# A decoder trunk on one core: the mixer's instruction order, the engine of the pooling sums and the buffers of the second values

## The reference

```
h = x + 1/2 * postRMS(SwiGLU_1(preRMS(x)))
u = preRMS(h); a = u @ w_in
y = [conv_module(a_conv) | multiscale_pool(a_pool) | sparse_attention(a_q, a_k, a_v, a_qidx, a_kidx, a_widx)] @ w_out
h = h + postRMS(y)
h = h + 1/2 * postRMS(SwiGLU_2(preRMS(h)))
```

## Time and profile before

| | |
|---|---|
| runs | 1202.85, 1202.2 and 1207.68 us, median 1202.85 |
| profiled execution | 1207.4 us, span of its trace 1205.9 us |
| granted TensorE clock, mean | 0.958 of full speed |
| TensorE busy | 1112.4 us (92% of the span) |
| VectorE, ScalarE, GpSimd busy | 758.3, 529.6 and 220.4 us |
| bytes moved | 192.93 MB, mean 160 GB/s |
| first mixer | from about 220 to 395 us of the span, second from about 811 to 985 |

### The profile page before, as it was taken

The page is one execution under the profiler, slowest core; times in us unless marked ns, Lnnn a source line. Parts: engine busy times, 40 slices in busy tenths (PEclk is TensorE's granted clock), DMA queues, the critical chain, the costliest instruction groups (busy, mean ns, idle before and its releaser), DMA issues.

```text
span 1205.9 us, 28753 instructions
## 1 busy us (share of the span) xinstructions
PE 1112.4 (92%) x9404; PEld 1044.6 (87%) x9404; DVE 758.3 (63%) x1232; ACT 529.6 (44%) x854; POOL 220.4 (18%) x249
## 2 busy tenths in 40 slices
PE   5999999989579999999989999999885799999997
PEld 4999999877348899999989999998753699999995
DVE  3766644787854766664466666457788466666546
ACT  4444434521255544443454444345113555444335
POOL 3211100420600312110031111013224021211002
PEclk9999999999769999999999999999896799999999
DMA  7454566342553345555435456553336434555541
GB/s 248 170 204 169 196 230 225 114 124 98 105 151 128 106 174 187 178 189 177 157 91 194 179 196 225 207 193 109 103 105 111 131 123 157 182 183 183 183 174 39
DMA packets 92300, 192.93 MB, mean 160 GB/s; under 512 B 12338, under 2 KB 50418, under 8 KB 92098
## 3 DMA queue, kind: packets, MB, share of 16 engines
q1 hardware_dynamic: 89730, 187.44, 46.8%
q0 software_dynamic: 2496, 4.55, 1.7%
HBM read 189.35 MB, written 2.59 MB: 159 GB/s over the span
## 4 chain that ended last, share of the span: by engine, by line
PE 50%; issue 38%; DVE 3%; POOL 3%; ACT 2%; POOLq 2%; DMA 1%; DVEq 0%; ACTq 0%; SPq 0%
PE PS L999 14%; PE PS L1000 13%; PE PS L1001 13%; PE PS L1105 3%; PE PS L1033 2%; POOLq L1465 1%; PE PS L1044 1%; PE PS L1048 1%; PE PS L1045 1%; POOL h L1420 1%; ACT w_hi L356 1%; POOL pa L1472 1%; DVE w_lo L559 1%; DVE wk L684 1%; PE PS L1111 1%
## 5 line engine op out<-in xcount | busy, mean ns | idle before, releaser
L559 DVE TENSOR_TENSOR w_lo<-raw,w_hi 128x1024 fp32r<-128x1024 f32 x300 | 395.3, 1318 | 315.1 <-ACT w_hi L356 313.1
L356 ACT ACTIVATE w_hi<-raw 128x1024 fp32r<-128x1024 f32 x300 | 315.7, 1055 | 256.0 <-PE PS L1001 221.3
L999 PE MATMUL PS<-x_hi,w_hi 128*128 128x264 f32 x1456 | 417.0, 286 | 10.8 <-DVE w_lo L559 10.8
L1000 PE MATMUL PS<-x_lo,w_hi 128*128 128x264 f32 x1456 | 414.7, 285 | 0.0
L1001 PE MATMUL PS<-x_hi,w_lo 128*128 128x264 f32 x1456 | 414.3, 285 | 0.0
L999 PEld LDWEIGHTS PS<-x_hi,w_hi 128*128 128x128 f32 x1456 | 276.3, 190 | 12.0 <-DVE w_lo L559 11.7
L1000 PEld LDWEIGHTS PS<-x_lo,w_hi 128*128 128x128 f32 x1456 | 276.5, 190 | 0.1
L1001 PEld LDWEIGHTS PS<-x_hi,w_lo 128*128 128x128 f32 x1456 | 275.2, 189 | 0.0
L999 PE MATMUL PS<-h_hi,w_hi 128*128 (+1 forms) x832 | 237.1, 285 | 3.4 <-issue 3.0
L1001 PE MATMUL PS<-h_hi,w_lo 128*128 (+1 forms) x832 | 236.9, 285 | 0.0
L1000 PE MATMUL PS<-h_lo,w_hi 128*128 (+1 forms) x832 | 236.2, 284 | 0.0
(11 more groups left out here) (265 smaller groups left out, 1072.2 us busy)
## 6 DMA issues: line engine op xcount, KB each, us to landing
raw<-in_wts SPq DMA_DIRECT2D x315, 512.0 KB, 3.6
kv<-in_kT SPq DMA_DIRECT2D x128, 64.0 KB, 2.2
kx<-in_kxT SPq DMA_DIRECT2D x128, 32.0 KB, 2.1
kv<-in_vC SPq DMA_DIRECT2D x64, 64.0 KB, 1.9
vx<-in_vC POOLq DMA_DIRECT2D x32, 64.0 KB, 2.3
vx<-in_vC SPq DMA_DIRECT2D x32, 64.0 KB, 2.1
h<-in_xT SPq DMA_DIRECT2D x1, 1056.0 KB, 5.0
out_yT<-h SPq DMA_DIRECT2D x8, 132.0 KB, 1.7
```

Source lines behind the costliest of these rows:

```text
L356: act.activation(w_hi[:, u % SPLIT, :], raw[:, u % RAW, :], ACT.Copy) \
L559: tt(w_lo[:, u % SPLIT, :], raw[:, u % RAW, :], w_hi[:, u % SPLIT, :].bitcast(F32), AL.subtract) \
L999: pe.matmul(out, w_hi[:, w, cols], hi, start=start, stop=False)
L1000: pe.matmul(out, w_hi[:, w, cols], lo, start=False, stop=False)
```

## The change

It reorders the mixer's middle, on all engines:

1. **Digits one unit later.** `plain(9)` goes ahead of `rope(ak)`, and TensorE runs `digit(i)` after `whole(10 + i)` instead of ahead of it. The trial value of the next digit is prepared in `count` (`ahead`), so that one operation is left behind a digit's arrival instead of three. `digit(7)` moves from behind `masked(0)` to ahead of it.
2. **First scores ahead of the sample keys.** TensorE runs `scores(0)`, `fold`, `keys(0)`, `scores(1)` instead of `fold`, `keys(0)`, `scores(0)`, `scores(1)`. The match of the new key (`new_key`) moves to the last round.
3. **Layer norm between prompt rounds.** The sums `c_sum` and `c_var` run in bank 6 behind `scores(1)` and inside round 0; centring, square, root and scaling go with them.
4. **VectorE pools.** GpSimd's window sums go to VectorE, in two parts (`windows_2_and_4` ahead of the softmax's normalisation, `windows_8_and_16` behind it). GpSimd keeps the stores.
5. **Second values in weight buffers.** The odd values of sequences 1, 3 and 5 go into slots 3, 4 and 5 of `raw`, the first two as soon as unit 17 is split; only the last goes to `kv`. Units 21 to 23 wait until `values(1)` is done. The first values of sequence 2 are loaded by GpSimd, which now starts 24 page loads instead of 16.
6. ScalarE copies `pTs` behind the SiLU and its rounding instead of ahead of them.

```diff
@@ SyncE
-                    if n >= end - 6:
-                        read((1, 3, 5, 7, 0, 2)[n - end + 6])
+                    if end - 6 <= n < end - 1:
+                        read((1, 3, 5, 7, 0)[n - end + 6])
+
+                sp.wait_ge(sem["w_hi"], end + 3 - RAW)
+                sp.wait_ge(sem["w_lo"], end + 3 - RAW)
+                spare_values(L, 0, places)
+                spare_values(L, 1, places)
+                for q in range(KV):
+                    batch(kT, L, q, places[2 * q + 1], "k_used", q + 1)
 
                 sp.wait_ge(sem["unit_done"], at_layer(L, "unit_done", U_MIX + N_IN - 1))
                 first_values(L, 0, places)
-                for q in range(KV):
-                    batch(kT, L, q, places[2 * q + 1], "k_used", q + 1)
-
-                first_values(L, 1, places)
-                for q in range(KV):
-                    batch(vC, L, q, places[2 * q + 1], "k_used", KV + q + 1)
+                spare_values(L, 2, places)
+                batch(vC, L, 3, places[7], "k_used", KV + 4)
+
+                sp.wait_ge(sem["v_used"], at_layer(L, "v_used", 2))
                 for n in range(end, L * UNITS + U_FFN2):
                     unit(n)
@@ ScalarE
                 exps(0)
                 for j in range(4):
-                    if j < 3:
+                    if j == 0:
+                        exps(1)
+                        act.wait_ge(sem["c_cent"], at_layer(L, "c_cent", 1))
+                        act.activation(csq[:, :, :], cacc[:, :, :], ACT.Square).then_inc(sem["c_sq"], 1)
+                    elif j < 3:
                         exps(j + 1)
...
+                    if j == 0:
+                        act.wait_ge(sem["c_var"], at_layer(L, "c_var", 1))
+                        act.activation(crs[:, :], PS[:, 6, 0:NT], ACT.Sqrt, scale=1.0 / 256,
+                                       bias=epsb[:, 0:1]).then_inc(sem["c_rms"], 1)
@@ VectorE
                 def count(i):
 
-                    if i == 0:
-                        linked(tt(trial, prefix, radi[:, 0:1], AL.bitwise_or))
-                    linked(ts(ties[:, :], Z[:, :], trial.bitcast(F32), 0.0, AL.is_ge, AL.add, accum_out=cnt))
+                    at_least = trial if i else radi[:, 0:1]
+                    linked(ts(ties[:, :], Z[:, :], at_least.bitcast(F32), 0.0, AL.is_ge, AL.add, accum_out=cnt))
                     tt(reach, cnt, rank, AL.is_ge).then_inc(sem["count"], 1)
-
-                def digit(i):
-
+                    if i == len(SHIFTS) - 1:
+                        return step(L, tt(prefix, prefix, found, AL.bitwise_or))
+                    if i:
+                        linked(tt(prefix, prefix, found, AL.bitwise_or))
+                    if i < len(SHIFTS) - 1:
+                        return step(L, tt(ahead, prefix, radi[:, i + 1:i + 2], AL.bitwise_or))
+
+                def digit(i, prepared=None):
+
+                    if prepared:
+                        after(L, prepared)
                     dve.wait_ge(sem["digit"], at_layer(L, "digit", i + 1))
                     unit = 2.0 ** SHIFTS[i]
                     linked(ts(found, PS[:, 6, 448 + i:449 + i], unit if SHIFTS[i] else 0.5, -unit, AL.mult, AL.add))
                     if i < len(SHIFTS) - 1:
-                        tt(trial, found, radi[:, i + 1:i + 2], AL.bitwise_or)
-                    linked(tt(prefix, prefix, found, AL.bitwise_or))
-                    if i < len(SHIFTS) - 1:
-                        linked(tt(trial, trial, prefix, AL.bitwise_or))
+                        linked(tt(trial, found, ahead, AL.bitwise_or))
+                    else:
+                        linked(tt(prefix, prefix, found, AL.bitwise_or))
...
+                def windows_2_and_4():
+
+                    dve.wait_ge(sem["pool_c"], at_layer(L, "pool_c", 1))
+                    a = step(L, tt(pa[:, 0:270], pp[:, 0, 0:270], pp[:, 0, 1:271], AL.add))
+                    b = step(L, tt(pb[:, 0:270], pp[:, 1, 0:270], pp[:, 1, 1:271], AL.add))
+                    for g in range(4):
+                        rows, w = slice(64 * (g % 2), 64 * (g % 2) + 64), 2 << g
+                        dve.tensor_reduce(pw[rows, g // 2, NP:], stp[rows, g // 2, :, PB + 1 - w:], AX.X, AL.add)
+                    after(L, a)
+                    tt(pw[64:128, 0, 0:NP], pa[64:128, 12:12 + NP], pa[64:128, 14:14 + NP], AL.add)
+                    after(L, b)
+                    return step(L, tt(pc[:, 0:268], pb[:, 0:268], pb[:, 2:270], AL.add))
...
                 masked(0)
                 above()
                 masked(1)
                 norm(0)
+                centred()
                 ranked = equals()
                 norm(1)
                 masked(2)
                 selected = chosen(ranked)
                 heads_out(0)
                 norm(2)
                 masked(3)
+                normalized()
                 heads_out(1)
                 norm(3)
                 heads_out(2)
-                heads_out(3)
...
                 ts(smx[:, 1:2], smx[:, 0:1], -SCALE, None, AL.mult).then_inc(sem["s_smax"], 1)
+                heads_out(3)
+                fours = windows_2_and_4()
                 dve.wait_ge(sem["p_sexp"], at_layer(L, "p_sexp", 1))
                 after(L, step(L, dve.reciprocal(smx[:, 3:4], smx[:, 2:3])))
                 ts(psm[:, :], psm[:, :], smx[:, 3:4], None, AL.mult).then_inc(sem["p_snorm"], 1)
                 dve.wait_ge(sem["p_snorm"], at_layer(L, "p_snorm", 1))
                 ts(heads(dg[:, :]), own_rows, psm[:, PAST:], None, AL.mult).then_inc(sem["dg"], 1)
...
+                windows_8_and_16(fours)
@@ TensorE
-                pe.wait_ge(sem["v_nat"], at_layer(L, "v_nat", 1))
-                digit(0)
                 whole(10)
                 pe.wait_ge(sem["rope"], at_layer(L, "rope", 4))
                 perm(9, aq[:, 0, :], 2).then_inc(sem["perm"], 1)
-                digit(1)
+                pe.wait_ge(sem["v_nat"], at_layer(L, "v_nat", 1))
+                digit(0)
...
-                fold()
...
+                scores(0)
+                fold()
                 keys(0)
-                scores(0)
                 scores(1)
+                pe.wait_ge(sem["conv_p"], at_layer(L, "conv_p", 1))
+                pe.wait_ge(sem["conv_s"], at_layer(L, "conv_s", 1))
+                pe.wait_ge(sem["v_nat"], at_layer(L, "v_nat", 1))
+                channel_sum(cacc, "c_sum")
@@ GpSimd
-                    for q in (2, 3):
+                    for q in (1, 2, 3):
```

203 lines of the change are left out of this document (100 added, 103 removed).

## The result

The changed kernel takes **1174.95 us** (median of 4 runs, 1174.59 to 1176.05) against 1204.76 for the kernel before (1202.2 to 1207.68) on the same chip: a ratio of 0.9745, with a 95% interval of 0.9726 to 0.9765. The profiled execution took 1174.9 us (span 1173.0, before 1205.9), at a mean granted clock of 0.980 (before 0.958). The sum was made for this execution, and there it said 1187.4: it is 12.5 us off, and only the 4.5 that were taken off for the median make it look like 8.

What follows compares the result with a forecast made beforehand. Inside the mixers the path was taken to run through VectorE, with TensorE half idle and often at lower clock. Terms -8.6, -1.8, -2.9, +1.3, +2.0 gave -10.0 a layer: 1187.4 us profiled, 1183 against the median, range 1175 to 1193.

Steps and rivals of the forecast that it cites:

- The likeliest case: The forecast itself: -10.0 us a layer, 1183 us against the median, own range 1180 to 1187, chance 0.42.
- The first rival: First keys at full clock or second-key pages all in time: -13.4 us a layer, 1176 us; chance 0.27.
- Digits and first scores: Transposes to `scores(1)`: unit 10 starts earlier, small waits remain, `scores(1)` starts at once: -8.6 us a layer.
- `fold` and `keys(0)` follow at their old distances: After the digits: taps, copies and first keys keep their spacing, so `keys(0)` ends at 308.0, 5.4 us earlier.
- Rounds 0 to 2: 318.44 to 335.63: VectorE without GpSimd's contention gains 3.4; centring, second channel sum and table load cost some: -1.8 us a layer.
- The 0.5 for the table load: In rounds 0 to 2: the exponentials' table load after the root is hidden except for 0.5 us.
- Round 3: From round 3 to the sample softmax: less work stands between `keys(1)` and the softmax, -2.9 us a layer.
- Second keys: At `keys(1)`: last pages fall just behind GpSimd's store; wait of 0 to 7 us, taken as +2.0 a layer.
- Softmax to the end: From softmax to `values(1)`: `windows_2_and_4` overruns VectorE's wait for the exponential, +1.3 us a layer, bounds 0 and +3.
- VectorE was not too full: Rival: late keys with the scaling and second windows bare, -0.5 us a layer, 1202 us; chance 0.05.
- the weights did not come late: Rival: units 21 to 23, loaded behind `values(1)`, arrive too late and make the kernel slower; chance 0.03.
- the table loads did not stand bare: Rival: both table loads for the root unhidden in the rounds, 2.1 us a layer more, 1187 us; chance 0.03.

Runs made afterwards that it cites:

- both orders back: Changed kernel with the digits one unit earlier again and the first scores behind the first keys again: 1193.69 us.
- the norm at the end: Changed kernel with the layer norm of the convolved channels moved back behind round 3 on all engines: 1184.21 us.
- the earlier store: Changed kernel with GpSimd's store of the pool state issued one group of three page loads earlier: 1187.04 us.

## Why the prediction fell short

The likeliest case was the wrong one. The first rival, "the lower clock stays away, or the pages slip past the store", gave 1176 and had 0.27; it came true in both halves. That its 1176 lies within 1.1 us of the median is luck: its sum had -13.4 a layer and 1180.6 for the profiled execution, and measured are -15.8 and 1174.9. By the steps, the 5.8 us a layer that the sum lacks are 1.2, 0.9, 1.0, 1.8, 0.1 and 0.8 in the order of the table:

*Digits and first scores: mechanism right, one size off.* The three small waits (0.4, 0.9, 0.8 forecast; 0.39, 0.94, 0.48 measured), the start of unit 10 and its full clock came as written. The step that failed is "`fold` and `keys(0)` follow at their old distances": the keys took 1.90 us and not 3.41, so the term is -9.8, beside the -10.0 that the text gave for this case. I argued against it from a clock of 0.76 in the next stretch. The run with both orders back shows that such a stretch does not settle it: 1.90 and 3.40 behind the same wait in one execution.

*Rounds 0 to 2: -2.7 instead of -1.8.* Small operations and pairs ran uncontended as forecast; no run prices that in this place. The 0.5 for the table load was too much: "If the load were done ahead of the wait it costs nothing" was the case. The drain behind each load, by which the step would have cost more, is not in these rows. Centring cost 1.0 and not 0.7, by the run with the norm at the end. The 0.7 us that remain are not settled.

*Round 3: -3.9 instead of -2.9.* The work taken out was timed by its instructions; the run that puts it back brings the 11.2 us of this step back in full, with 5.9 us of VectorE's idle time in it. That these waits between the engines are what the estimate missed is argued from the rows.

*Second keys: "I take +2.0" is the step that failed, with the largest share.* It measured 0.2 and 0. The range of 0 to 7 and its reason were right, as the earlier store shows (5.2 and 7.3). But the two issue times on which it hung were 1.0 to 1.8 us apart in a sum of terms each uncertain by about as much. That half a us decides was nearly right: landing goes from 2.6 to 9.1 us within 1.5 us behind the start of the store. But +2.0 does not follow from it: with the last page 1.0 to 1.8 behind the store, as forecast, those rows give a landing of 6.6 to 9.1 us and a wait of 4.5 to 7. (The text's own terms, 286.2 + 26.2 and eight loads of 1.4 to 1.5, give 323.6 to 324.4 for the store and not 323.3 to 324.1, so 0.7 to 1.5.) And the first keys' clock, which I had left open, moved one of them: with `keys(0)` at the full clock the key loads started at 306.5 instead of the 308.2 of the forecast, and the last one was issued 1.1 ahead of the store in the first mixer and 0.3 in the second. The two were one case, and I had given its halves a lower chance together than the case that needed both to fail.

*Softmax to the end: right.* +1.2 for +1.3. The matrices behind `values(0)` ran at the full clock from 345.0 on, -0.8, another gain of the clock.

Not of the sum: of the 1.9 us outside the mixers, 1.4 are the two values between which the last stretch jumps whatever the edit, and the kernel before had the long one. Of the other rivals nothing came: VectorE was not too full, the weights did not come late, the table loads did not stand bare.

Do the parts add? By the ratios, put back one at a time, they cost 9.8, 12.0, 8.3, 2.9 and 2.5, together 35 where the whole change brought 30, and digits and scores together cost 16.8 and not 21.8. By the mixers of the profiled executions they cost 9.5, 5.1, 9.4, 3.2 and 1.3, together 28.4 of 31.6, and digits and scores together 16.2 beside 14.6. The two differ most for the first scores, whose other runs took longer than the profiled one. So the parts add within what these measurements can tell, and with the second keys' waits, up to 2.5 us, inside most of them.

## What to carry to other kernels

A store like this one (120 KB, 10 to 12 us to land) makes the loads issued behind it slow for about as long, so its place is a choice like that of any other work: here behind the last load that something waits for, and not in the stretch where TensorE issues hundreds of small matmuls. Where TensorE must wait on the path for a few us and the work right behind it is on the path too, fill the wait with matmuls that nobody reads; first see in the profile that the work behind runs at half the clock. And when two terms of a forecast depend on the same open question, here the clock of the first keys, they are one case and not two.

## What the runs showed of the hardware

- The same matmuls behind the same wait ran at 2.4 GHz in one mixer and at 1.2 in the other of one execution (16 matmuls in 1.90 and 3.40 us). Outside the mixers, too, one drop comes or stays away: before, TensorE's clock is 0.51 at 1002.5 to 1004.5 (row below) behind a wait of 1.92 us; after, the same wait ends at 970.05 and the clock stays at 1.00. The stretches with the drop are some 1.5 us longer.

```profile
1002.50:1004.50 2.00, 2.00 (x12) 2.00 (x11) 0.84 (x2) 1.12 (x2) 1.12 (x1) 0.51 0.83 272
```

- Stand-in matmuls in a wait of 5.5 us held the clock: 1.93 us instead of 3.60 for the 64 matmuls behind it.
- A store of 120 KB took 10.1 to 11.9 us to land, and pages of 64 KB issued behind it 8.7 us instead of 2.1.
- Behind such a store TensorE issued 36 small matmuls in 4 us instead of 172, waiting for nothing that the profile names.
- A table load was started ahead of its instruction's wait: of its 1.28 us, 0.33 and 0.98 stood behind the end of the wait in the two mixers, and neither was on the path.
